# A two-block transformer kernel on one Trainium2 core: routing weights before ranks, attention steps between chunk halves, one weight chunk and one context load in another place

## The reference

```
# first block (one layer)
h  = modulate(rms_norm(x), sh1, sc1)          # sh, sc, gt: silu(c) @ ada_w
x  = x + gt1 * (merged retention and hyena branches) @ w_out
h2 = modulate(rms_norm(x), sh2, sc2)
x  = x + gt2 * moe_ffn(h2)                    # 32 experts in 4 groups, top 2 of one group
x  = rms_norm(x)
# second block (two layers)
for l in range(2):
    p, pc = h @ w_in[l], hc @ w_in[l]         # hc: the context stream
    y  = concat[fourier_mix, neighbourhood attention, spatial gating, differential attention] @ w_out[l]
    if l == 0:                                # the context's own layer
        cx = cx + cg1 * (same four groups on the context) @ w_out[0]
        cx = cx + cg2 * relu(hc2 @ w_ff1[0])**2 @ w_ff2[0]
    x = x + g1 * y
    x = x + g2 * relu(h2 @ w_ff1[l])**2 @ w_ff2[l]
return rms_norm(x)
```

## Time and profile before

| | us |
|---|---|
| median of 3 runs | 1851.88 |
| lowest and highest | 1850.9, 1856.36 |
| the profiled execution, its own time | 1854.06 |
| its span, first to last instruction | 1852.3 |
| TensorE busy in it | 1770.3 (96%) |
| TensorE's mean granted clock | 0.993 of full |
| VectorE, ScalarE busy | 465.0, 318.7 |
| bytes moved | 470.84 MB, mean 254 GB/s |

### The profile page before, as it was taken

The page is one execution under the profiler, slowest core; times in us unless marked ns, Lnnn a source line. Parts: engine busy times, 40 slices in busy tenths (PEclk is TensorE's granted clock), DMA queues, the critical chain, the costliest instruction groups (busy, mean ns, idle before and its releaser), DMA issues. The chain is left out here.

```text
span 1852.3 us, 24570 instructions
## 1 busy us (share of the span) xinstructions
PE 1770.3 (96%) x10852; PEld 1345.6 (73%) x10852; DVE 465.0 (25%) x1012; ACT 318.7 (17%) x722; POOL 0.2 (0%) x4
## 2 busy tenths in 40 slices
PE   5999999999998999999999999899999999999997
PEld 3674887887663566666666686688888876788886
DVE  4410124535024221110101245422100134411001
ACT  4110013104114111010000125221100134111000
POOL 0000000000000000000000000000000000000000
PEclk9999999999999999999999999899999999999999
DMA  9353666567899999999999952287544231454430
GB/s 381 163 227 116 232 233 240 189 243 305 356 376 392 422 421 421 421 421 421 420 421 421 397 182 92 80 336 267 197 146 157 73 112 63 178 212 151 146 112 23
DMA packets 61522, 470.84 MB, mean 254 GB/s; under 512 B 7687, under 2 KB 11176, under 8 KB 12008
## 3 DMA queue, kind: packets, MB, share of 16 engines
q1 hardware_dynamic: 60184, 467.98, 64.6%
q10 hardware_dynamic: 1232, 1.28, 0.2%
HBM read 468.19 MB, written 1.05 MB: 253 GB/s over the span
## 5 line engine op out<-in xcount | busy, mean ns | idle before, releaser
L2460 PE MATMUL bank<-hT,ring 128*128 128x256 f32 x1024 | 222.3, 379 | 0.0
L2483 PE MATMUL bank<-second_work,ring 128*128 128x256 f32 x1024 | 221.3, 379 | 0.0
L2483 PEld LDWEIGHTS bank<-second_work,ring 128*128 128x128 f32 x1024 | 194.6, 190 | 26.5
L2460 PEld LDWEIGHTS bank<-hT,ring 128*128 128x128 f32 x1024 | 194.3, 190 | 26.1
L1321 PE MATMUL bank<-hT,ring 128*128 128x256 f32 x672 | 153.4, 385 | 7.1 <-DMA ring<-in_w_ff 4.4
L1321 PEld LDWEIGHTS bank<-hT,ring 128*128 128x128 f32 x672 | 126.8, 192 | 40.7 <-issue 12.9
L631 PE MATMUL bank<-hT,ring 128*128 128x256 f32 x704 | 153.5, 379 | 0.0
L631 PEld LDWEIGHTS bank<-hT,ring 128*128 128x128 f32 x704 | 133.5, 190 | 18.9 <-issue 1.2
L1754 PE MATMUL bank<-ring,rowsT 128*32 128x512 f32 x1008 | 116.8, 596 | 0.8 <-DMA ring<-in_expert_w 0.6
L1321 PE MATMUL bank<-tmp,ring 128*128 128x256 f32 x384 | 87.2, 382 | 10.1 <-DMA ring<-in_w_ff 6.3
L1321 PEld LDWEIGHTS bank<-tmp,ring 128*128 128x128 f32 x384 | 71.7, 190 | 29.9 <-DMA ring<-in_w_ff 13.4
(11 more groups left out here) (467 smaller groups left out, 1697.4 us busy)
## 6 DMA issues: line engine op xcount, KB each, us to landing
ring<-in_expert_w SPq DMA_DIRECT2D x190, 1024.0 KB, 12.9
ring<-in_w_ff SPq DMA_DIRECT2D x96, 1024.0 KB, 7.2
ring<-in_ada_w SPq DMA_DIRECT2D x36, 2048.0 KB, 8.6
ring<-in_w_in SPq DMA_DIRECT2D x27, 1024.0 KB, 7.2
ring<-in_w_in SPq DMA_DIRECT2D x13, 2048.0 KB, 11.1
ring<-in_w_out SPq DMA_DIRECT2D x12, 1024.0 KB, 6.7
ring<-in_ret_w_o SPq DMA_DIRECT2D x2, 2048.0 KB, 8.4
ring<-in_w_out SPq DMA_DIRECT2D x2, 2048.0 KB, 13.0
```

The source lines that it names most:

```text
L2460: mm = pe.matmul(ff_bank(n), w[:, k, (n % 2) * P:(n % 2 + 1) * P], hT[:, k, xs], start=k == 0, stop=k == DT - 1)
L2483: mm = pe.matmul(ff_bank(FT + i), w[:, f, :], W[:, 16 * h + f, :], start=h == f == 0, stop=h == 1 and f == FT // 2 - 1)
```

## The change

- **Context load.** SyncE's `load_ahead` ahead of the load of `ctx2T` goes only up to the first chunk of `ret_w_o`, so the load of the `ada_w_2` chunk that the second one frees comes behind `ctx2T`.
- **Routing.** VectorE's 7 instructions for the weights stand ahead of the wait for `ranked`; the reduction for the flag comes behind the ranks; the other flag instructions and `over` stand between the two halves of `picked_w`. TensorE reads the flag after the first two groups of transposes.
- **Attention steps.** The first of each two attention steps moves ahead of the piece's second half: `ctx_pe_between` runs it between the two chunks, `ctx_pe_beside` the other one.
- **Context out-product.** The first one does 6 of its 8 products ahead of the wait for `post`.
- **Layer 0, x stream.** One `ada_w_2` chunk is loaded ahead of `w_out_2` and multiplied in attention step 12 into bank 2; the other chunks of `gating` move up by one place, so that the feed-forward has four.

```diff
             if l == 0:
+                plan_both("ada2_gap", [wide("ada_w_2", 1, 1)], [], [0])
+            plan_both(f"out2_{l}", [wide("w_out_2", j, l, n=GW) for j in range(4)], [wide("ada_w_2", (2, 7)[l], 1)],
                       [0, 1, 0, 0])
             if l == 0:
-                plan_both("ada2_rest", [wide("ada_w_2", j, 1) for j in range(2, 4)], [], [0] * 2)
+                plan_both("ada2_rest", [wide("ada_w_2", j, 1) for j in range(3, 5)], [], [0] * 2)
                 plan_both(f"ff1_{l}", [wide("w_ff1_2", j, l, n=GW) for j in range(16)],
-                          [wide("ada_w_2", j, 1) for j in (4, 5, 6, 8, 9)], [0] + [0, 1] * 5 + [0] * 5)
+                          [wide("ada_w_2", j, 1) for j in (5, 6, 8, 9)], [0] + [0, 1] * 4 + [0] * 7)
...
-                            load_ahead(sp, at["ret_o"][0] + 1)
+                            load_ahead(sp, at["ret_o"][0])
                             sp.wait_ge(S("mix_tile"), MIX)
                             sp.dma_start(cT[:, :, :], a["ctx2T"]).then_inc(S("ctx_loaded"), 16)
...
                         pe.wait_ge(K("y"), 4)
+                        ctx_tile(pe, OUT_TILE, [(w[:, k, m], yT_c[:, k, :]) for k in range(6)], 0, 2)
                         pe.wait_ge(K("post"), 1)
-                    ctx_tile(pe, OUT_TILE + n, [(w[:, k, m], yT_c[:, k, :]) for k in range(DT)])
+                        ctx_tile(pe, OUT_TILE, [(w[:, k, m], yT_c[:, k, :]) for k in (6, 7)], 1, 2)
...
+            def ctx_pe_between(pe, g, n):
+                if 0 <= 4 * g + n - CTX_ATTEND < 8:
+                    attend_pe(pe, 2 * (4 * g + n - CTX_ATTEND))
...
                 if 0 <= 4 * g + n - CTX_ATTEND < 8:
-                    for s in range(2 * (4 * g + n - CTX_ATTEND), 2 * (4 * g + n - CTX_ATTEND) + 2):
-                        attend_pe(pe, s)
+                    attend_pe(pe, 2 * (4 * g + n - CTX_ATTEND) + 1)
...
                             for k in range(2):
+                                if k == 1:
+                                    ctx_pe_between(pe, 3 * q + m, n)
...
-                        pe.wait_ge(S("flag_ready"), 1)
-                        flagged = pe.value_load(flag_i[0:1, 0:1], min_val=0, max_val=1)
                         for n in range(QUADS // 2):
+                            if n == 2:
+                                pe.wait_ge(S("flag_ready"), 1)
+                                flagged = pe.value_load(flag_i[0:1, 0:1], min_val=0, max_val=1)
...
                         for s in range(len(TILES[l]) - ATTEND_AT[l], STEPS_X):
+                            if l == 0 and s == UNITS:
+                                pe.wait_ge(S("exp"), 2 * (UNITS - 1))
+                                gating.pe(pe, 0)
```

More of the change, by code:

```diff
@@ L348, in build, with __init__ @@
         class Modulations:
-            def __init__(self, jobs, sums, turned, part, ident, tag="ada"):
+            def __init__(self, jobs, sums, turned, part, ident, tag="ada", first_sum=None):
                 self.jobs, self.sums, self.turned, self.part, self.ident = jobs, sums, turned, part, ident
@@ L359, in __init__, with sum_bank @@
                 self.depth = len(sums)
+                self.first_sum = sums[0] if first_sum is None else first_sum
+            def sum_bank(self, c):
+                return self.sums[c % self.depth] if c else self.first_sum
             def pe(self, pe, c, turns=True):
@@ L391, in act @@
                     act.wait_ge(S(self.turns), c - self.depth + 1)
-                nc.scalar.copy(self.part[c % self.depth][:, 0:P], self.sums[c % self.depth][:, 0:P]).then_inc(S(self.parted), 1)
+                nc.scalar.copy(self.part[c % self.depth][:, 0:P], self.sum_bank(c)[:, 0:P]).then_inc(S(self.parted), 1)
             def dve(self, dve, c):
@@ L1385, in ctx_pe @@
                         pe.wait_ge(K("y"), 4)
+                        ctx_tile(pe, OUT_TILE, [(w[:, k, m], yT_c[:, k, :]) for k in range(6)], 0, 2)
                         pe.wait_ge(K("post"), 1)
-                    ctx_tile(pe, OUT_TILE + n, [(w[:, k, m], yT_c[:, k, :]) for k in range(DT)])
+                        ctx_tile(pe, OUT_TILE, [(w[:, k, m], yT_c[:, k, :]) for k in (6, 7)], 1, 2)
+                    else:
+                        ctx_tile(pe, OUT_TILE + n, [(w[:, k, m], yT_c[:, k, :]) for k in range(DT)])
                     if i % 2 == 1:
@@ L2095, in _ @@
                         do(nc.vector.reciprocal(sc(2), sc(2)))
-                        dve.wait_ge(S("ranked"), 1)
-                        do(nc.vector.scalar_tensor_tensor(out=rank, in0=bank[4][:, 0:64].rearrange("p (t e) -> p t e", t=TT),
-                                                          scalar=1.0, in1=chosen[:, :, :], op0=ALU.add, op1=ALU.mult))
-                        do(ts(rank, rank, -1.0, None, ALU.add))
-                        per_e = lambda x: x.rearrange("p (e a) -> p e a", a=1).to_broadcast([P, EXPERTS, CAP])
-                        row_no = C0("iota").rearrange("p (a c) -> p a c", a=1).to_broadcast([P, EXPERTS, CAP])
-                        for t in range(TT):
-                            do(tt(pick[:, t, :].rearrange("p (e c) -> p e c", c=CAP), row_no, per_e(rank[:, t, :]), ALU.is_equal))
                         dve.wait_ge(S("gap_exp"), 1)
@@ L2113, in _ @@
                         do(tt(weight[:, :, :], one1, one2, ALU.add))
-                        do(ts(over[:, :, :], rank, float(CAP), None, ALU.is_ge))
+                        dve.wait_ge(S("ranked"), 1)
+                        do(nc.vector.scalar_tensor_tensor(out=rank, in0=bank[4][:, 0:64].rearrange("p (t e) -> p t e", t=TT),
+                                                          scalar=1.0, in1=chosen[:, :, :], op0=ALU.add, op1=ALU.mult))
+                        do(ts(rank, rank, -1.0, None, ALU.add))
                         do(nc.vector.tensor_reduce(flag[:, :], bank[4][:, 64:96], AX_X, ALU.max))
-                        do(ts(flag[:, :], flag[:, :], float(CAP), None, ALU.is_gt))
-                        do(nc.vector.tensor_copy(flag_i[:, :], flag[:, :]), "flag_ready")
+                        per_e = lambda x: x.rearrange("p (e a) -> p e a", a=1).to_broadcast([P, EXPERTS, CAP])
+                        row_no = C0("iota").rearrange("p (a c) -> p a c", a=1).to_broadcast([P, EXPERTS, CAP])
+                        for t in range(TT):
+                            do(tt(pick[:, t, :].rearrange("p (e c) -> p e c", c=CAP), row_no, per_e(rank[:, t, :]), ALU.is_equal))
                         for h in range(2):
@@ L2123, in _ @@
                             i.then_inc(S("picked"), 1)
+                            if h == 0:
+                                do(ts(over[:, :, :], rank, float(CAP), None, ALU.is_ge))
+                                do(ts(flag[:, :], flag[:, :], float(CAP), None, ALU.is_gt))
+                                do(nc.vector.tensor_copy(flag_i[:, :], flag[:, :]), "flag_ready")
                         do(tt(over[:, :, :], over[:, :, :], weight[:, :, :], ALU.mult))
@@ L2269, in ada_after @@
                 m = n - 5
-                return [3 + m // 4] if l == 0 and 0 <= m < 20 and m % 4 == 0 else []
+                return [4 + m // 4] if l == 0 and 0 <= m < 16 and m % 4 == 0 else []
             def store(sp):
@@ L2506, in _ @@
                         if l == 0:
-                            for n in range(1, 3):
+                            for n in range(2, 4):
                                 gating.pe(pe, n)
@@ L2589, in shifted @@
                             if k == 1 and chunks is not None:
-                                chunks.act(act, 2)
+                                chunks.act(act, 3 if chunks is gating else 2)
                     for l in range(LAYERS):
@@ L2608, in _ @@
                                     nc.scalar.copy(yT[:, j, :], bank[j][:, 0:T]).then_inc(S("four"), 1)
+                            if l == 0 and s == UNITS:
+                                gating.act(act, 0)
                             attend(l, s)
@@ L2622, in _ @@
                         root(2 * l + 1)
[L2623 to L2626 removed]
+                        (gating, gating_last)[l].act(act, 2 - l)
                         shifted(mod, 24, 16 * l, (gating, gating_last)[l])
```

20 lines of the change are left out of this document (10 added, 10 removed).

## The result

| | before | after |
|---|---|---|
| median | 1853.54 us (7 runs) | 1843.43 us (7 runs) |
| lowest and highest | 1850.9, 1856.36 | 1841.01, 1848.02 |
| the profiled execution, its own time | 1854.06 | 1843.16 |
| its span | 1852.3 | 1841.4 |
| mean granted clock | 0.993 | 0.995 |

The ratio after to before is 0.9946, 95% interval 0.9931 to 0.9961: faster, by 10 us in the medians and 10.9 in the two profiled spans. The forecast was 1842.4 in a range of 1838 to 1848.5, with 9.5 us for the difference. It was taken off the median of three executions, 1851.88; off the 1853.54 of seven it would be 1844.0. How far the terms are right too has to be read from the places.

A forecast was written before the change was run, and what follows sets the result against it. TensorE is busy 96%, but the weight stream at 421 GB/s was taken to bound the experts' stage, moving only by its holes. Terms 1.8 + 2.6 + 2.5 + 0 + 2.0 + 0.6 = 9.5 us off 1851.88 gave 1842.4, range 1838 to 1848.5.

The forecast's parts named there:

- Context, -1.8: Context load: ctx2T comes about 5 us sooner, so TensorE's 1.84 us wait for the sum goes; -1.8, between 0 and 1.84.
- Routing, -2.6: Routing: the first half of picked_w comes 2.2 us sooner and its transposes probably run at the upper clock; -2.6 us.
- Attention steps, -2.5: Context's attention: half pieces fill waits, freeing w2 slots sooner; the stream's 2.8 us hole at 594 takes 2.5 us.
- That the stream is last: About 555 to 1018 us: weight loads at 421 GB/s set the pace; removed TensorE waits return as chunk waits.
- the hole at 494: Load stream at 494 to 496 us, nothing moved: it hands the context and routing gains, 4.4 us, on in full.
- Out-product, 0: Context's out-product: the 1.8 us wait for L1656 goes, but the stream runs at 421 GB/s around it; gain 0.
- A rival: TensorE counts in full, everywhere: all removed waits count, 15.9 us, 1836.0; at the out-product -1.8; chance 0.04.
- Tail, -2.0 for the chunk: Layer 0's tail: a chunk fills the 2.10 us wait at no cost, and the feed-forward loses one chunk; -2.0 us.
- Tail's clock, -0.6: Behind layer 0's filled tail wait: the clock, 0.50 for 3.5 us, may stay up; -0.6, between 0 and -1.75.
- the clock stays up everywhere: Rival: shorter waits keep TensorE at 2.4 GHz, at the gather too; 11.2 us gained, 1840.7; chance 0.19.
- The stage's end doesn't move: Rival: gains in and ahead of the experts return as chunk waits; only 2.6 us left, 1849.3; chance 0.20, including under-half moves.
- slower: Rival: short bursts drop TensorE's clock for the whole attention, +19.3 there, +9.8 net, 1861.7; chance 0.04.

The follow-up runs named there:

- the first execution: The changed kernel as first profiled against the kernel before: median 1843.43 us (7 runs), ratio 0.9946, span 1841.4.
- the kernel with thin loads: The kernel before with the experts' chunks from the second quad on loaded at half their bytes: 1833.84 us, ratio 0.9896.
- the filler: The kernel before with 64 useless matmul instructions in the 2.10 us wait of layer 0's tail, nothing taken away: 1853.46 us, ratio 0.9997.
- the second execution: The changed kernel run and profiled once more, nothing edited: 1841.25 us (4 runs), ratio 0.9929 to the kernel before, span 1841.8.
- the further step's kernel: The changed kernel with half of layer 0's token transform moved ahead of a 1.61 us wait: 1843.22 us, ratio 0.9937 to the kernel before.

## Why the prediction was right, step by step

- **Context, -1.8: right.** -2.0 (13.81 against 15.76 to 16.12 us in the eight executions with the wait). Missed was what goes with it: in four of these eight the clock fell there, 1.6 to 2.1 us more. The earlier trace rows happened to show one in which it did not, and I took "after 1.84 us of waiting not slow" as a property of the wait. It is one throw.
- **Routing, -2.6: mechanism right, size a little small.** The halves came 2.1 and 1.6 us sooner against the ranks, as worked out. To the first gather it is -2.76, and since the gather itself had been slow too, -3.0 to the second (82.26 against 85.25); -1.4 where the clock falls (83.89).
- **Attention steps, -2.5: mechanism right, parts off, the size near by some luck.** At the third gather -2.06: -0.5 up to the wait of 1.95 (0.8 forecast), -2.55 to the last transposes (2.7), +1.0 at the hidden rows (1.1). The forecast had the gather behind it slow as before; in the first execution it ran at the upper clock and gave another 1.63, in the second it was slow. The stream took less than TensorE had won in both: D grew by 1.5 and 1.0 us, and 2.2 and 1.2 are left at the stage's end. The hole was 3.3 us, not 2.8, since the earlier trace rows leave out 598 to 600 (315 GB/s); it is closed in the first and about half closed in the second. In the first 0.6 us of transfer are lost anew from 680 to 700 (408 GB/s), behind the fall near 670.
- **That the stream is last: shown**, by the kernel with thin loads (no wait for a chunk, -19 us) and by the out-product alone (0, its 1.8 back as waits for `w_out`). That it moves only by its holes fits the traces (the hole comes back without the steps, and the end with it), but is shown less well: the kernel with the steps alone gained nothing. Where my text said that the hole at 494 hands on the gain in full, the hole moved forward with its size about kept (53, 0 and 70 GB/s in three windows of 2 us before, 303, 20, 29 and 254 in four after), and it handed on most: of the routing's 3.0 the kernel with the routing alone keeps 2.5 from the router's first product to the stage's end (609.7 against 612.2).
- **Out-product, 0: right.** A rival would have had 1.8.
- **Tail, -2.0 for the chunk: right**, 2.1 by six executions against eight.
- **Tail's clock, -0.6: the step that was mis-sized.** It is -1.26, and the filler gives it by itself. The mechanism was right, also that VectorE's normalisation takes back a part: 1.54 us, as the wait for L2751. What was too small is the stretch: I counted the 3.5 us of the transform, but the lower clock held from 1171.4 to 1177.5, 6.1 us at 0.51. The transposes ahead of the transform gave 0.43, the transform 1.64 less the 1.54, the gating units 0.74. The wait for `post` went from 0.79 to 0.54 because one transpose more lies in it, as worked out.

The sum of the terms as measured in the first pair: 2.0 + 3.0 + 2.2 (steps at the stage's end) + 0 + 2.1 + 1.3 = 10.6; 0.3 more are from ahead of the change, and A and E together give 0. In the second execution the same places give 2.0 + 1.4 + 1.2 + 0 + 2.1 + 1.3 = 8.0, and E (1.7) and what lies ahead of the change (0.9) bring the span to 10.5 under the one before again. So that the total came so near to 9.5 both times owes something to luck with the clock. The rival "the clock stays up everywhere" (1840.7) describes the profiled execution at the routing and the hidden rows but not in E, and the second execution not even there. The Trainium skill, "TensorE: Matmul & The Clock Gate", section "HAM oscillation — how this bites in real kernels", has long waits between bursts let the clock drop, so that the next burst starts slow. At 3.35 us the traces agree in 9 of 9, though in four of them only after eight fast transposes. At the shorter waits, which the rule there doesn't cover, the clock fell too: in 10 of 14 at 2.75 us and in 18 of 28 at 1.6 to 2.1 us (A, E and the empty tail). So neither "slow" nor "not slow" was the right forecast there, but a chance for each.

"The stage's end doesn't move" and "slower" are out: it moved by 5.4 and 7.4 us, and the clock did not fall for the attention as a whole.

## What to carry to other kernels

Ask of each wait whether the stream of loads or the engine is last around it, and count a removed wait only up to the hole that it can close: taking away 1.8 us of waiting was worth 0 in the experts' stage (the out-product) and its full time ahead of it (the context's sum). Work put into a wait pays twice where the clock would fall behind it, but only if that work's own inputs aren't queued behind what the engine is waiting for. And where parts of 2 us hide in times that scatter by 9, compare the length of fixed stretches over all traces that there are; here those that no edit touched repeated, or differed by a fall of the clock.

## What the runs showed of the hardware

- The granted clock after a wait of 1 to 2 us is not fixed by the program. The two executions of the changed kernel, with the same waits at the places that the table names, differ in where the clock fell: the first near 670 us (5.0 us for what took 3.5 in the second) and at E, the second at the routing and the hidden rows.
- A fall can reach the stage's end even where the stream is last. In the further step's kernel a product group behind the wait of 2.75 us took 6.71 us instead of 3.7 to 5.4; from 680 to 700 the stream carried 370 GB/s, against 408 and 422 in the two executions of the changed kernel, and D is 456.1 us against 454.1 and 453.6. That the slots which the group frees came late is my reading of it, from one execution. Timeline of that kernel:

```profile
669.96 6.71 PE L1327 MATMUL bank<-hT,ring 128*128 128x256 f32 x16 [2.75 <-issue]
```

- The stream shows no reserve over 421 GB/s: from 740 to 1040 us it carries 421 in the kernel before and in both executions of the changed one, wherever each stands, so nothing of a hole is made up there.
- Waits for chunks have a usual size in this stage: 1.40 to 1.43 us in 7 of 15 rows before and in 10 of 17 after; the others are 0.2 to 1.6.
